# Weight units in seventeen homes, tokens gathered for two experts at once, and a hinted loop over pairs

## The chip, the cores and the metric

The kernel runs on one core of a Trainium2 chip. The metric is the device time of one execution in microseconds (us). Several executions are timed and their median is reported. One more execution is recorded by the hardware profiler; its trace covers the span from the first to the last instruction.

## The reference

One layer of a diffusion backbone, in float32, for 128 context tokens and 256 latent tokens of width 1024: a state-space mixer with a gated linear unit, then a mixture of experts, then a final norm. The change lies in the mixture of experts:

```
scores = sigmoid(t @ router_w)                 # 384 tokens, 16 experts
top_w, top_idx = two experts for each token    # both from one group of four
g = t @ w_gate[e];  u = t @ w_up[e]            # each 1024 x 1024
y += combine[e] * ((silu(g) * u) @ w_down[e])  # 1024 x 1024
x = x + g2 * y;  out = rms_norm(x) * norm_final
```

All sixteen experts are evaluated, each on those tokens that chose it. Their weights are 16 x 3 matrices of 4 MiB. The 384 tokens make 768 choices, so an expert has 48 tokens on average.

## The kernel before, in words

There is no scheduler: each engine has its own program, and counting semaphores order them. The code is named by its functions and lines.

**Weights.** An expert's weights are 12 units of 1 MiB, each loaded by two DMAs of 512 KB from SP's queue. Units 0 to 7 hold 128 rows of `w_gate` and of `w_up`; units 8 to 11 hold 256 rows of `w_down`. They live in `ring`, which has twelve slots (L102), unit u of every expert in slot u. TensorE raises `unit_free` after its last use of a unit, in the order 0 to 11 (in `expert`, L1327 to L1374), and SP's `load_unit` (L430) then loads the next expert's unit into that slot. Before the loop starts, SP loads all of E0 and also five units of E1 (0 to 4) into memory that other data has left (`early_unit`, L228, `load_early`, L450). VectorE copies these five into the ring when E0 has used the slots (L1879 to L1882), and SP goes on with unit 5. Experts are called E0 to E15 here.

**TensorE's loop** (L1400) runs over sixteen experts. Up to 96 tokens of an expert are held as three tiles of 32; the third is computed only if the expert has more than 64. One pass of `expert` does this, in order:

1. if over 64: the third tile's gate and up (`third_gate_up`) over all units 0 to 7;
2. gate and up of tiles 0 and 1, unit by unit, each 32 tokens by 512 columns on a quarter of the array (`gate_up`, L1307);
3. the first part of the gather for the next expert (`gather_x`, L1295, its five first k of eight);
4. transposes of the activations (L1357);
5. the rest of the gather;
6. if over 64: the third tile's down; then the down of tiles 0 and 1 (`down`, L1314), which use units 8 to 11.

**The gather** turns token rows into columns: for each of eight blocks k of 128 channels, three matmuls with a 128x128 block of `h2` as weights and 96 columns of a one-hot matrix (`onehot`) moved. VectorE makes the one-hot matrix (`find_tokens`, L1772) and copies the result from two PSUM banks into `xgT` (`evict_x`, L1838). E0's gather stands before the loop (`gather_first`, L1376).

**Rows out.** ScalarE applies SiLU and copies transposes; ScalarE and VectorE copy the down results into `yrow`; GpSimd scatters these to a scratch tensor `y2_scratch` in HBM. The last expert's rows stay on the chip: after the loop TensorE spreads them to tokens with matmuls (L1421).

**The end.** When the rows of E14 are sent, SP reloads the scratch in six DMAs (`load_y2`, L471), behind the weights on the same queue. ScalarE weights the first choice of each third of the tokens (`first_choice`, L845), VectorE adds the second, the gate and the residual in three steps of 1024 columns each (`other_choice`, L1843). VectorE's program has these behind its products of E15; ScalarE's has the first of them before, and the other two after, the copies of E15's last down results. Then come `combine` (L1909), the norm and the stores. If any expert had over 96 tokens, further rounds would run (L1403 on); TensorE jumps over that code.

Of the kernel before, what the change touches and what calls it, by code (L numbers as in the profile page):

```python
# [71 lines left out]
NU = 12  # L72
MAGIC = 12582912.0
# [12 lines left out]
def build(nc, x_prompt, x_sample, c, state_re, state_im, c_ctx, norm_mix, norm_ffn, w_ada, b_ada,  # L86
# [7 lines left out]
    with ctx:  # L94
# [71 lines left out]
        def cut(region, n):  # L166
# [46 lines left out]
        onehot = cut(vreg, NT * CAP).rearrange("p (t n) -> p t n", t=NT)  # L213
# [3 lines left out]
        xgT = cut(vreg, KT * CAP).rearrange("p (k t) -> p k t", k=KT)  # L217
# [6 lines left out]
        sig = cut(vreg, 512)  # L224
        prod = cut(vreg, 512)
        gfin = cut(vreg, D)
        assert off[0] <= 2 * DG * NP_V * GS
        early_unit = [mod2[:, 0, :, :].rearrange("p r n -> p (r n)"), mod2[:, 1, :, :].rearrange("p r n -> p (r n)"),  # L228
                      h2T[:, :, :].rearrange("p k t -> p (k t)")[:, 0:UNIT],
                      tmat[:, :, :].rearrange("p g n -> p (g n)"), front[:, :]]  # L230
        yo = ring[:, 8:10, :].rearrange("p a b -> p (a b)")[:, 0:NT * D].rearrange("p (t n) -> p t n", t=NT)
        y2c = [mod2[:, :, :, :].rearrange("p a r n -> p (a r n)")[:, 0:NT * D].rearrange("p (t n) -> p t n", t=NT),
               h2T[:, :, :].rearrange("p k t -> p (k t)").rearrange("p (t n) -> p t n", t=NT)]
# [5 lines left out]
        def back_of(t, j):  # L239
# [41 lines left out]
        st_zero, dve_oh_last, pe_oh_last, act_oh_last, dve_pre, pe_back, dve_oh_none, dve_mix = (sem(n) for n in (  # L281
            "st_zero", "dve_oh_last", "pe_oh_last", "act_oh_last", "dve_pre", "pe_back", "dve_oh_none", "dve_mix"))
        ld_early = [sem(f"ld_early{u}") for u in range(len(early_unit))]
# [27 lines left out]
        def first_piece(half, k):  # L311
            return ring[:, FIRST_UNITS[4 * half + k // 2], 1024 * (k % 2):1024 * (k % 2) + 1024].rearrange(
                "p (s n) -> p s n", s=2)

# [9 lines left out]
        def _(sp):  # L324
# [105 lines left out]
            def load_unit(u, e):  # L430
                if u < KT:
                    for h, w in enumerate((w_gate, w_up)):
                        sp.dma_start(ring[:, u, h * D:(h + 1) * D],  # L433
                                     w[0, bass.ds(e, 1), u * P:(u + 1) * P, :].rearrange("a p n -> (a p) n")
                                     ).then_inc(ld_unit[u], 16)
                else:
                    for h in range(2):
                        k = 2 * (u - KT) + h
                        sp.dma_start(ring[:, u, h * D:(h + 1) * D],
                                     w_down[0, bass.ds(e, 1), k * P:(k + 1) * P, :].rearrange("a p n -> (a p) n")  # L440
                                     ).then_inc(ld_unit[u], 16)

            sp.wait_ge(pe_yT, 6)
            for u in (0, 1, 5):
                load_unit(u, 0)
            for n, u in enumerate((2, 3, 6, 7, 8, 9, 10, 11, 4)):
                sp.wait_ge(glu_free, min(n + 1, KT))
                load_unit(u, 0)

            def load_early(u):  # L450
                for h, w in enumerate((w_gate, w_up)):
                    sp.dma_start(early_unit[u][:, h * D:(h + 1) * D], w[0, 1, u * P:(u + 1) * P, :]
                                 ).then_inc(ld_early[u], 16)
            load_early(4)
            sp.wait_ge(dve_x1, 6)
            load_early(3)
            sp.wait_ge(dve_h2, 6)
            load_early(0)
            load_early(1)
            sp.wait_ge(pe_logit, NT)  # L460
            load_early(2)
            for u in range(len(early_unit), NU):
# [1499 lines left out]
```

## Time and profile before

| | |
|---|---|
| median of 3 runs | 830.61 us (828.04 to 834.56) |
| the profiled execution | 827.5 us, span 825.8 us |
| mean granted clock of TensorE | 0.953 |
| TensorE matmul, weight load busy | 748.5 us (91%), 413.5 us (50%) |
| VectorE, ScalarE, GpSimd busy | 311.3 (38%), 187.7 (23%), 46.6 (6%) |
| DMA, mean over the span | 261.05 MB, 316 GB/s |

In a window row the busy times are those of TensorE, its weight loads, VectorE, ScalarE and GpSimd, in this order. The expert loop takes the span from 320.9 us to 798.3 us. Shares of the whole span mix stages with different limits, so the stages are read one at a time, with windows (busy time in a stretch) and with the instructions in order of time. Each float32 matmul shows as two matmul records and two weight-load records. Four matmuls on quarters of the array run side by side, so 128 records of them are 32 in a row.

### The profile page before, as it was taken

The page shows a single profiled execution, that of the slowest core. Times are in us where ns is not written, and L with a number is a line of the kernel's source. Part 1 is how long each engine was busy: PE and PEld are TensorE (multiplying, and loading weights), DVE is VectorE, ACT ScalarE, POOL GpSimd, SP SyncE. Part 2 cuts the span into 40 slices and gives each one's busy share as a digit, 9 for nine tenths or more (in the row PEclk, how much of TensorE's full clock was granted, in tenths as well). Part 3 has the DMA queues.
Part 4 walks back from the last instruction along what each step waited for, and adds up shares of the span by engine and source line. Part 5 has one row for each costly group of instructions (what it writes and reads, how often), then busy time and mean ns, then how long its engine had stood idle before and what let it go on. Part 6 is the DMA issues. An engine that isn't in the chain of part 4 may idle for free.

```text
span 825.8 us, 22906 instructions
## 1 busy us (share of the span) xinstructions
PE 748.5 (91%) x9776; PEld 413.5 (50%) x9777; DVE 311.3 (38%) x808; ACT 187.7 (23%) x394; POOL 46.6 (6%) x102
## 2 busy tenths in 40 slices
PE   6999788689899979999998999999999999999862
PEld 6455454484554466554552654454554554454232
DVE  6779869996022176211120211111201211121138
ACT  5535330210141133212220212201201212220132
POOL 2000300000010002100000000000000000000000
PEclk9999998959999977999999999999999999999986
DMA  9920569910059991799999999999999999999981
GB/s 329 393 80 2 204 219 397 373 40 35 22 188 348 324 376 48 272 413 409 411 410 411 410 411 411 410 410 411 410 410 379 412 410 410 411 410 410 410 332 77
DMA packets 73227, 261.05 MB, mean 316 GB/s; under 512 B 10668, under 2 KB 10716, under 8 KB 70104
## 3 DMA queue, kind: packets, MB, share of 16 engines
q1 hardware_dynamic: 71032, 257.17, 79.5%
q0 software_dynamic: 1552, 2.99, 0.9%
q8 instruction: 40, 0.66, 0.3%
q10 hardware_dynamic: 592, 0.14, 0.1%
q14 instruction: 11, 0.09, 0.0%
HBM read 252.49 MB, written 9.17 MB: 317 GB/s over the span
## 4 chain that ended last, share of the span: by engine, by line
PE 66%; DVE 16%; DMA 8%; SPq 6%; issue 3%; ACT 1%; DVEq 0%; ACTq 0%
PE ps L1311 23%; PE ps L1318 11%; PE ps L1303 8%; PE ps L1217 7%; DMA ring<-in_moe_w_up 6%; SPq L433 5%; DVE sreg L1678 3%; PE ps L1277 3%; PE ps L1153 3%; DVE scan_t L1670 3%; DMA vreg<-y_scratch 2%; PE ps L1033 2%; PE ps L1090 2%; DVE sreg L1559 2%; PE ps L1378 1%
## 5 line engine op out<-in xcount | busy, mean ns | idle before, releaser
L1311 PE MATMUL ps<-ring,vreg 128*32 128x512 f32 x2240 | 245.6, 593 | 13.1 <-DMA ring<-in_moe_w_up 8.3
L1311 PEld LDWEIGHTS ps<-ring,vreg 128*32 128x32 f32 x2240 | 72.3, 110 | 179.4 <-issue 160.9
L1318 PE MATMUL ps<-ring,vreg 128*32 128x256 f32 x2240 | 125.8, 383 | 0.8 <-ACT vreg L857 0.8
L1855 DVE TENSOR_TENSOR vreg<-vreg,ps 128x256 f32<-128x256 f32 x48 | 17.3, 417 | 212.2 <-ACT vreg L852 212.2
L1318 PEld LDWEIGHTS ps<-ring,vreg 128*32 128x32 f32 x2240 | 71.4, 111 | 49.1 <-issue 2.9
L1303 PEld LDWEIGHTS ps<-vreg,sreg 128*128 128x128 f32 x720 | 82.7, 192 | 12.6 <-issue 12.6
L1303 PE MATMUL ps<-vreg,sreg 128*128 128x96 f32 x720 | 86.0, 276 | 0.0
L1873 DVE COPY vreg<-ps 32x256 f32<-32x256 f32 x90 | 38.1, 423 | 99.6 <-PE ps L1318 97.2
L874 ACT ACTIVATE vreg<-ps 32x256 f32<-32x256 f32 x90 | 33.6, 373 | 139.4 <-PE ps L1318 137.6
L852 ACT ACTIVATE vreg<-ps 128x256 f32<-128x256 f32 x48 | 15.0, 385 | 196.3 <-PE ps L1311 196.3
L1217 PE MATMUL ps<-ring 128*128 128x512 f32 x128 | 57.8, 610 | 1.5 <-issue 0.7
L1678 DVE TENSOR_TENSOR sreg<-sreg,scan_t 128x128 f32<-128x128 f32 x190 | 47.9, 313 | 2.1
L1033 PE MATMUL ps<-ring,sreg 128*128 128x512 f32 x96 | 43.6, 601 | 1.0 <-DVE sreg L1591 1.0
L1217 PEld LDWEIGHTS ps<-ring 128*128 128x128 f32 x128 | 24.5, 194 | 31.2 <-issue 30.1
L1670 DVE TENSOR_TENSOR scan_t<-a,sreg 128x256 f32<-128x256 f32 x95 | 38.4, 445 | 1.1
L1840 DVE COPY vreg<-ps 128x480 f32<-128x480 f32 x16 | 10.5, 658 | 71.9 <-PE ps L1303 69.5
L1153 PE MATMUL ps<-sreg,vreg 64*64 64x32 f32 (+1 forms) x1024 | 25.3, 265 | 5.9 <-issue 3.6
L1033 PEld LDWEIGHTS ps<-ring,sreg 128*128 128x128 f32 x96 | 17.5, 190 | 22.5 <-issue 22.0
L1153 PEld LDWEIGHTS ps<-sreg,vreg 64*64 64x64 f32 x1024 | 24.1, 180 | 8.3 <-issue 6.1
L1277 PE MATMUL ps<-ring 128*128 128x512 f32 x64 | 27.6, 592 | 0.0
L571 POOL TENSOR_TENSOR pool_tick<-ident 1x1 f32<-1x1 f32 x30 | 5.5, 183 | 388.1 <-DVE vreg L1873 308.8
L1713 DVE TENSOR_TENSOR vreg<-vreg,ps 128x512 f32<-128x512 f32 x4 | 2.8, 688 | 52.2 <-DMA sreg<-in_x_prompt 38.0
(306 smaller groups left out, 642.3 us busy)
## 6 DMA issues: line engine op xcount, KB each, us to landing
ring<-in_moe_w_down SPq DMA_DIRECT2D x128, 512.0 KB, 12.1
ring<-in_moe_w_gate SPq DMA_DIRECT2D x123, 512.0 KB, 13.1
ring<-in_moe_w_up SPq DMA_DIRECT2D x123, 512.0 KB, 14.3
ring<-in_w_ada SPq DMA_DIRECT2D x16, 1024.0 KB, 7.5
ring<-in_w_ada SPq DMA_DIRECT2D x16, 512.0 KB, 11.8
ring<-in_ssm_w_glu SPq DMA_DIRECT2D x8, 1024.0 KB, 12.9
ring<-in_ssm_w_in SPq DMA_DIRECT2D x8, 512.0 KB, 12.3
y_scratch<-sreg SPq DMA_DIRECT2D x6, 512.0 KB, 7.1
```

What stands on the lines that cost most here:

```text
L433: sp.dma_start(ring[:, u, h * D:(h + 1) * D], w[0, bass.ds(e, 1), u * P:(u + 1) * P, :].rearrange("a p n -> (a p) n")).then_inc(ld_unit[u] ...
L874: act.activation(yrow[32 * t:32 * t + 32, 256 * j:256 * j + 256], src, ACT.Copy).then_inc(y_ev, 1)
L1033: last = pe.matmul(ps[4 + m % 4][:, :], hT[:, k, (m // 2) * P:(m // 2 + 1) * P], win[:, k, (m % 2) * 512:(m % 2 + 1) * 512], start=(k == 0 ...
L1153: last = pe.matmul(y_out(bank_of(i), i, n, o, cols), v, states_of(a, d, r, g, first_col - 1 + 2 * d, cols), start=False, stop=(d == 1 and ...
L1217: last = pe.matmul(ps[GLU_BANK[m] + part][:, :], lhs, ring[:, GLU_SLOT[k], col:col + 512], start=(k == 4), stop=(k == 3))
L1277: last = pe.matmul(ps[GLU_BANK[m] + part][:, :], yT_lat[:, k, P:2 * P], ring[:, GLU_SLOT[k], col:col + 512], start=(k == 4), stop=(k == 3))
L1303: last = pe.matmul(bank[:, col * CAP:(col + 1) * CAP], h2[:, t, k * P:(k + 1) * P], onehot[:, t, :], start=(t == 0), stop=(t == NT - 1))
L1311: last = pe.matmul(ps[t][32 * j:32 * j + 32, :], xgT[:, k, 32 * t:32 * t + 32], w[:, :, 256 * j:256 * j + 256], start=(k == 0), stop=(k == ...
L1318: last = pe.matmul(ps[3 + t // 2][32 * dj:32 * dj + 32, 256 * (t % 2):256 * (t % 2) + 256], aT[:, t, c2, 32 * j:32 * j + 32], ring[:, KT + ...
L1670: step(tt(scan_t[:, st, :, :].rearrange("p x (d g) -> p x d g", d=2), A4, chunk_states(f[st] - 1, b[st] + 1, "xdg"), ALU.mult), False)
L1678: step(tt(to, to, tb, ALU.add), False)
L1873: cp(yrow[32 * t:32 * t + 32, 256 * j:256 * j + 256], src).then_inc(y_ev, 1)
```

## The change

Three things are edited, and what depends on them.

- **Homes.** Units 0 to 6 keep one slot each in the ring. Units 7 to 11 get two homes: the ring for even experts, and for odd experts the memory that had held the early units (`odd_unit`), with semaphores of their own. That is seventeen homes. Ahead of the loop SP loads E0 and units 7 to 11 of E1, with the same waits as the early units had. In the loop SP loads units 7 to 11 of an expert first (their home was used by the expert two before) and then 0 to 6. VectorE's copies are gone. Of unit 8 the second half is loaded first. The reload of the rows goes to ring slots 8 to 10, the outputs are built in slots 0 and 1.
- **Gather.** TensorE's loop runs over eight pairs, with both experts written out in its body. A one-hot matrix for two experts (192 columns) is moved at once: half of the eight k in the even expert of a pair, the other half in the odd one, for the next pair. E0 and E1 are still gathered one by one; E1's gather stands in E0, followed by a wait until VectorE has copied it out. The last pair gathers nothing. VectorE copies out in four copies a pair, each when the odd expert has used the k that it overwrites.
[...]

The diff at its core (the rounds after the first, and signatures that only pass `odd` on, are left out):

```diff
+SINGLE = 7
+PAIRS = NE // 2
...
+        odd_unit = [front[:, :], tmat[:, :, :].rearrange("p g n -> p (g n)"),
+                    mod2[:, 0, :, :].rearrange("p r n -> p (r n)"), mod2[:, 1, :, :].rearrange("p r n -> p (r n)"),
...
+        def unit_of(u, odd):
+            return odd_unit[u - SINGLE] if odd and u >= SINGLE else ring[:, u, :]
+        yo = ring[:, 0:2, :].rearrange("p a b -> p (a b)")[:, 0:NT * D].rearrange("p (t n) -> p t n", t=NT)
+        y2c = [ring[:, 8:11, :].rearrange("p a b -> p (a b)")[:, c * NT * D:(c + 1) * NT * D].rearrange(
+            "p (t n) -> p t n", t=NT) for c in range(2)]
...
+            def load_unit(u, i, odd):
+                def of_pair(w):
+                    return w[0].rearrange("(i two) p n -> two i p n", two=2)[int(odd), bass.ds(i, 1)]
+                for h in ((1, 0) if u == KT else (0, 1)):
+                    if u < KT:
+                        src = of_pair((w_gate, w_up)[h])[:, u * P:(u + 1) * P, :]
...
+                        src = of_pair(w_down)[:, k * P:(k + 1) * P, :]
+                    sp.dma_start(unit_of(u, odd)[:, h * D:(h + 1) * D], src.rearrange("a p n -> (a p) n")
+                                 ).then_inc(landed(u, odd), 16)
...
+            load_unit(7, 0, True)
...
+            def load_both(before, i, odd):
+                for u in range(SINGLE, NU):
+                    sp.wait_ge(unit_free, before + (int(odd) * NU + u + 1 - 2 * NU))
+                    load_unit(u, i, odd)
+                for u in range(SINGLE):
+                    sp.wait_ge(unit_free, before + (int(odd) * NU + u + 1 - NU))
+                    load_unit(u, i, odd)
+            for u in range(SINGLE):
                 sp.wait_ge(unit_free, u + 1)
-                load_unit(u, 1)
-            with sp.Fori(2, NE) as e:
-                for u in range(NU):
-                    sp.wait_ge(unit_free, e * NU + (u + 1 - NU))
-                    load_unit(u, e)
+                load_unit(u, 0, True)
+            with sp.Fori(1, NE // 2) as i:
+                for odd in (False, True):
+                    load_both(i * (2 * NU), i, odd)
...
+            def gather_one():
+                for k in range(KT):
                     bank, col = (ps[5], k) if k < 5 else (ps[6], k - 5)
                     for t in range(NT):
                         last = pe.matmul(bank[:, col * CAP:(col + 1) * CAP], h2[:, t, k * P:(k + 1) * P],
                                          onehot[:, t, :], start=(t == 0), stop=(t == NT - 1))
-                if end == KT:
+                last.then_inc(xt_ps, 1)
+
+            def gather_two(k0, end):
+                for k in range(k0, end):
+                    col = k % 2 * 2 * CAP
+                    for t in range(NT):
+                        last = pe.matmul(ps[5 + k % 4 // 2][:, col:col + 2 * CAP], h2[:, t, k * P:(k + 1) * P],
+                                         pair_hot[:, t, :], start=(t == 0), stop=(t == NT - 1))
+                if end % 4 == 0:
                     last.then_inc(xt_ps, 1)
...
+            def wait_unit(u, it, two, odd):
+                if u < SINGLE:
+                    pe.wait_ge(ld_unit[u], it * 32 + 32)
+                else:
+                    pe.wait_ge(landed(u, odd), two * 16 + 32)
...
-                with pe.If(e < NE - 1):
-                    gather_x(it + 1, 0, 5)
+                    wait_unit(k, it, two, odd)
+                    gate_up(k, 0, odd)
+                    gate_up(k, 1, odd).then_inc(unit_free, 1)
+                if not odd:
+                    with pe.If(i < 1):
+                        pe.wait_ge(oh_ready, r * (PAIRS + 1) + 2)
+                        gather_one()
+                        pe.wait_ge(single_ev, r * 2 + 2)
+                with pe.If(i < PAIRS - 1):
+                    if odd:
+                        pe.wait_ge(xt_ev, two * 2 + 6)
+                    else:
+                        pe.wait_ge(oh_ready, r * (PAIRS + 1) + i + 3)
+                    gather_two(4 * int(odd), 4 * int(odd) + 3)
...
-                with pe.If(e < NE - 1):
-                    gather_x(it + 1, 5, KT)
+                with pe.If(i < PAIRS - 1):
+                    gather_two(4 * int(odd) + 3, 4 * int(odd) + 4)
...
-            with pe.Fori(0, NE) as e:
-                n = pe.value_load(counts[0:1, bass.ds(e, 1)], min_val=0, max_val=T)
-                expert(e, e, n)
+            with nc.Fori(0, PAIRS, engines=[pe.engine], hint_back_edge=True) as i:
+                for odd in (False, True):
+                    n = pe.value_load(counts[0:1, bass.ds(i * 2 + int(odd), 1)], min_val=0, max_val=T)
+                    expert(0, i, odd, n)
...
+            def find_pair(e):
+                tt(pair_hot.rearrange("p t (e n) -> p t e n", e=2),
+                   posm[:, :, bass.ds(e, 2)].rearrange("p t (e n) -> p t e n", n=1).to_broadcast((P, NT, 2, CAP)),
+                   slot_no.rearrange("p (a b n) -> p a b n", a=1, b=1).to_broadcast((P, NT, 2, CAP)), ALU.is_equal
+                   ).then_inc(oh_ready, 1)
+
+            def evict_one(gathers, m, done):
+                dve.wait_ge(xt_ps, gathers)
+                cp(xgT[:, 0:5, m, :], ps[5][:, 0:5 * CAP].rearrange("p (k n) -> p k n", k=5)).then_inc(done, 1)
+                cp(xgT[:, 5:8, m, :], ps[6][:, 0:3 * CAP].rearrange("p (k n) -> p k n", k=3)).then_inc(done, 1)
+
+            def evict_two(gathers, k0, used):
+                dve.wait_ge(xt_ps, gathers)
+                for b in range(2):
+                    k = k0 + 2 * b
+                    dve.wait_ge(unit_free, used + k + 2)
+                    cp(xgT[:, k:k + 2, :, :], ps[5 + b][:, 0:4 * CAP].rearrange("p (k e n) -> p k e n", k=2, e=2)
+                       ).then_inc(xt_ev, 1)
 
             def other_choice(t, loads):
...
+            def even_expert(it, gathers=None):
+                products(it)
+                if gathers is not None:
+                    evict_one(gathers, 1, single_ev)
+                expert_rows(it)
+
+            def odd_expert(it, gathers, units, pair=None):
+                evict_two(gathers + 3, 0, units)
+                products(it)
+                evict_two(gathers + 4, 4, units)
+                if pair is not None:
+                    find_pair(pair)
+                expert_rows(it)
+            even_expert(0, 2)
+            with dve.Fori(0, PAIRS - 2) as i:
+                odd_expert(i * 2 + 1, i * 2, i * (2 * NU) + NU, i * 2 + 4)
+                even_expert(i * 2 + 2)
+            odd_expert(NE - 3, NE - 4, NU * (NE - 3))
+            even_expert(NE - 2)
+            products(NE - 1)
+            expert_rows(NE - 1, True)
```

## Rows read from the trace of the kernel before

**Rows 1.** five stretches: us, busy (records) by engine, granted clock, DMA share, GB/s

```profile
315.00:320.00 5.00, 4.49 (x25) 4.24 (x24) 2.43 (x9) 0.47 (x1) 0.00 (x0) 0.65 0.00 0
...
342.00:348.00 6.00, 6.00 (x112) 3.38 (x104) 0.39 (x2) 0.00 (x0) 0.18 (x1) 1.00 0.65 216
...
440.00:472.00 32.00, 31.52 (x386) 16.59 (x390) 2.66 (x7) 2.01 (x6) 0.36 (x2) 1.00 1.03 410
...
592.00:630.00 38.00, 37.68 (x443) 18.57 (x438) 5.08 (x13) 5.41 (x13) 1.47 (x4) 1.00 1.00 394
...
790.00:795.00 5.00, 5.00 (x72) 2.54 (x68) 0.00 (x0) 0.00 (x0) 0.00 (x0) 0.71 1.03 411
```

**Rows 2.** waits: engine, line, awaited: total us, times, longest

```profile
PE ps L1311 <- DMA ring<-in_moe_w_up: 8.3, 9, 1.8
```

**Rows 3.** order of time, E2: start, us, engine, line, records [idle before]

```profile
375.79 13.94 PE L1311 MATMUL ps<-ring,vreg 128*32 128x512 f32 x128 [0.28 <-issue]
...
389.66 3.59 PE L1303 MATMUL ps<-vreg,sreg 128*128 128x96 f32 x30
...
393.08 0.82 PE L1357 MATMUL ps<-ident,vreg 128*128 128x128 f32 x6
...
393.74 2.15 PE L1303 MATMUL ps<-vreg,sreg 128*128 128x96 f32 x18
...
395.82 7.11 PE L1318 MATMUL ps<-ring,vreg 128*32 128x256 f32 x128
...
403.19 0.64 PE L1311 MATMUL ps<-ring,vreg 128*32 128x512 f32 x4 [0.26 <-issue]
```

**Rows 4.** order of time, TensorE: experts with more than 64 tokens (E4, E9)

```profile
440.20 14.80 PE L1311 MATMUL ps<-ring,vreg 128*32 128x512 f32 x136 [1.79 <-DMA ring<-in_moe_w_up]
...
461.09 10.57 PE L1318 MATMUL ps<-ring,vreg 128*32 128x256 f32 x192
...
471.93 3.64 PE L1311 MATMUL ps<-ring,vreg 128*32 128x512 f32 x32 [0.28 <-issue]
...
592.31 20.81 PE L1311 MATMUL ps<-ring,vreg 128*32 128x512 f32 x192
```

**Rows 5.** order of time, TensorE, last expert

```profile
784.67 1.92 PE L1311 MATMUL ps<-ring,vreg 128*32 128x512 f32 x16 [0.64 <-DMA ring<-in_moe_w_up]
...
789.53 8.75 PE L1318 MATMUL ps<-ring,vreg 128*32 128x256 f32 x128 [0.80 <-ACT vreg L857]
```

**Rows 6.** order of time, chain of waits: matmuls before the loop

```profile
292.73 3.64 PE L1264 MATMUL ps<-sreg,vreg 128*128 128x16 f32 x32
...
250.82 13.73 PE ps L1217 x32
```

**Rows 7.** order of time, last steps before the loop, first after

```profile
319.20 0.66 DVE L1840 COPY vreg<-ps 128x480 f32<-128x480 f32 x1 [2.40 <-PE ps L1378]
...
320.87 13.94 PE L1311 MATMUL ps<-ring,vreg 128*32 128x512 f32 x128 [1.38 <-DVE vreg L1841]
...
797.46 1.15 ACT L847 ACTIVATE sreg<-sreg,cmb 128x1024 f32<-128x1024 f32 x1 [8.23 <-DMA vreg<-y_scratch]
...
803.70 1.15 ACT L847 ACTIVATE sreg<-sreg,cmb 128x1024 f32<-128x1024 f32 x1 [2.54 <-DMA vreg<-y_scratch]
...
803.89 5.50 PE L1421 MATMUL ps<-vreg,oh_rep 32*128 32x256 f32 x48 [5.60 <-issue]
...
808.73 1.23 DVE L1850 TENSOR_TENSOR sreg<-sreg 128x1024 f32<-128x1024 f32 x1
```

**Rows 8.** order of time, SP's queue: first loads after the seventeen

```profile
331.43 0.33 SPq L433 DMA_DIRECT2D ring<-in_moe_w_gate  x1
...
342.89 6.18 SPq L439 DMA_DIRECT2D ring<-in_moe_w_down  x8
```

**Rows 9.** the page: engine totals, instruction queue

```profile
PE 748.5 (91%) x9776; PEld 413.5 (50%) x9777; DVE 311.3 (38%) x808; ACT 187.7 (23%) x394; POOL 46.6 (6%) x102
...
q8 instruction: 40, 0.66, 0.3%
```

More of the change, by code:

```diff
@@ L313, in first_piece, with landed @@
                 "p (s n) -> p s n", s=2)
+        def landed(u, odd):
+            return ld_odd[u - SINGLE] if odd and u >= SINGLE else ld_unit[u]
         def of_half(i):
@@ L1294, in _ @@
                       start=False, stop=True, skip_group_check=True).then_inc(pe_pos, 1)
-            def gather_x(nth, first, end):
-                if first == 0:
-                    pe.wait_ge(oh_ready, nth + 1)
-                for k in range(first, end):
+            def gather_one():
+                for k in range(KT):
                     bank, col = (ps[5], k) if k < 5 else (ps[6], k - 5)
@@ L1335, in expert @@
-            def expert(it, e, count=None):
-                pe.wait_ge(xt_ev, it * 2 + 2)
+                        wait_unit(KT + kk // 2, it, two, odd)
+                    down(kk, 2, odd)
+            def expert(r, i, odd, count=None):
+                it = r * NE + i * 2 + int(odd) if count is None else i * 2 + int(odd)
+                two = r * NE + i * 2 if count is None else i * 2
+                pe.wait_ge(xt_ev, two * 2 + 4)
                 pe.wait_ge(prod_done, it * TT + TT)
                 if count is None:
-                    third_gate_up(it)
+                    third_gate_up(it, two, odd)
@@ L1363, in expert @@
                 if count is None:
-                    third_down(it)
+                    third_down(it, two, odd)
                 else:
                     with pe.If(count > 64):
-                        third_down(it)
+                        third_down(it, two, odd)
                 for kk in range(KT):
                     if kk % 2 == 0:
-                        pe.wait_ge(ld_unit[KT + kk // 2], it * 32 + 32)
-                    down(kk, 0)
-                    last = down(kk, 1)
+                        wait_unit(KT + kk // 2, it, two, odd)
+                    down(kk, 0, odd)
+                    last = down(kk, 1, odd)
                     if kk % 2:
@@ L1406, in _ @@
                     pe.wait_ge(xt_ev, r * (2 * NE))
-                    gather_x(r * NE, 0, KT)
-                    with pe.Fori(0, NE) as e:
-                        expert(r * NE + e, e)
+                    pe.wait_ge(oh_ready, r * (PAIRS + 1) + 1)
+                    gather_one()
+                    with nc.Fori(0, PAIRS, engines=[pe.engine], hint_back_edge=True) as i:
+                        for odd in (False, True):
+                            expert(r, i, odd)
                 pe.wait_ge(y_ev, 12 * NE * ROUNDS + 12)
@@ L1850, in other_choice, with products @@
                 tt(m, m, x1[:, t, :], ALU.add).then_inc(dve_pre, 1)
-            def expert(it, next_but_one, last_of_round=False, last=False):
+            def products(it):
                 for t in range(TT):
@@ L1855, in expert, with expert_rows @@
                     tt(act_a[:, t, :], sg[:, t, :], ps[t][:, 256:512], ALU.mult).then_inc(prod_done, 1)
[L1856 to L1859 removed]
+            def expert_rows(it, last=False):
                 if last:
@@ L1875, in _ @@
             dve.sem_inc(y_ev, 11)
-            evict_x(0)
+            evict_one(1, 0, xt_ev)
+            dve.sem_inc(xt_ev, 2)
             find_tokens(1)
+            find_pair(2)
             slot_numbers()
-            for u in range(len(early_unit)):
-                dve.wait_ge(ld_early[u], 32)
-                dve.wait_ge(unit_free, u + 1)
-                cp(ring[:, u, :], early_unit[u]).then_inc(ld_unit[u], 32)
-            with dve.Fori(0, NE - 2) as e:
-                expert(e, e + 2)
-            expert(NE - 2, None)
-            expert(NE - 1, None, True, True)
+            def even_expert(it, gathers=None):
[18 more added lines that the diff above has]
+            expert_rows(NE - 1, True)
             v = dve.value_load(cmaxi[0:1, 0:1], min_val=0, max_val=T)
```

114 lines of the change are left out of this document (43 added, 71 removed).

## The prediction

> **What bounds the kernel now.** I read the granted clock and DMA share by stretch first, then TensorE's waits, then the order of time on TensorE and on SP's queue. The expert loop is full on two resources at once. [...] TensorE's waits for weights add up to only 8.3 us over sixteen experts [rows 2]. DMA is idle just before the loop (nothing moves from 315 to 320) and a third idle from 342 to 348 [rows 1]. So what one resource gains can be taken back by the other, and both must be followed to the end.
>
> An expert of at most 64 tokens is 27.4 us of TensorE: gate and up 13.9, gather 3.5, transposes 0.7, gather 2.0, down 7.0, 0.3 of loop [rows 3]. Three experts (the fifth, eighth and tenth; I number them E4, E7, E9, from E0) have over 64 and take 10.4 more: 20.8 for 13.9, 10.6 for 7.1 [rows 3, 4]. One expert's weights are 12 units of 1 MiB. **Pace of the stream:** the last gate/up unit of E4 is used at 440.20 and that of E15 at 784.67, 132 units later [rows 4, 5]: 344.5 us. From 592 to 630 the DMA engines moved 394 GB/s for 410 [rows 1], a hole of 1.5 us. Without it 343.0/132 = 2.60 us a unit, the scatters of rows included, or 31.2 us an expert. An average expert of TensorE is 27.4 + 3 x 10.4/16 = 29.4. Weights are therefore the scarcer thing, and at the end of the loop TensorE waits for each unit.
>
> **The change part by part.**
>
> *Gather for two.* A 128x128 weight load with 16 columns moved takes 3.64/32 = 114 ns a record, and with 96 columns 3.59/30, that is 117 [rows 3, 6]: the load sets the time. Moving sets it for 512 columns (13.73/32 = 429 ns) and for 256 (four side by side, 4 x 7.11/128 = 222) [rows 3, 6]. For 192 columns: 192/512 x 429 = 161 or 192/256 x 222 = 167; the ends are 117 (the load still hides it) and 234 (two of today's). I take 167, the nearest width. A pair then costs 48 x 0.167 = 8.0 us for 11.0, half in each expert: a small expert falls from 27.4 to 26.0 (3.0 + 1.0 for 3.5 + 2.0). E0 carries in addition the single gather for E1 (48 x 0.117 = 5.6) and TensorE's new wait until DVE has emptied its two banks. Such an eviction took from 319.20 to the restart at 320.87, 1.7 us with the count's load [rows 3, 7]; I take 1.4. Behind that wait stand the pair's gather and E0's transposes and down; VectorE is free by then. E0 becomes 26.0 + 5.6 + 1.4 = 33.0. The last pair gathers nothing: E14 is 22.0. TensorE alone would end at 320.9 + 33.0 + 10 x 26.0 + 3 x 36.4 + 22.0 + 25.6 = 770.7, where 25.6 is E15's 13.9 and the 11.7 from its gates' end (784.67 + 1.92) to 798.28 [rows 5]. The loop ends at 798.3 now.
>
> *Seventeen homes.* As many units (17) are loaded ahead of the loop as before; VectorE's five copies go, and it has room anyway. What moves is the next load. Today unit 5 of E1 is issued at 331.43, after six units of E0 are used, and unit 8 of E1 at 342.89, after E0's first down unit; then the stream runs on with 20 units issued before it [rows 8]. After: unit 0 of E1 can go at 320.9 + 1.7 = 322.6, 8.8 us earlier. Eight units (0 to 6 of E1, 7 of E2) keep DMA busy to about 345. Unit 8 of E2 needs E0's first down unit, and E0 is longer: 320.9 + 13.9 + 5.6 + 1.4 + 3.0 + 0.7 + 1.0 + 1.9 = 348.4. DMA is idle for some 4 us, then runs on with 25 units behind it. The lead is 5 x 2.60 - (348.4 - 342.9) = 7.5 us. From then on I find no late home: the tightest are the down homes after the large experts, free 4 us before DMA wants them, so the 1.5 us hole goes too. The stream ends 9 us earlier.
>
> *The order of loads.* This takes it back. An expert's units 7 to 11 are now loaded before its 0 to 6. Today the stream's last gate unit is number 188 of 192 (7 of E15); after, the last of all is unit 6 of E15, and its gates stand behind it. By position: today's lag is 440.20 - 342.89 - 36 x 2.60 = 3.7; unit 6 of E15 is the 167th of the restarted stream, 348.4 + 167 x 2.60 + 3.7 = 786.3. I call this landing L15; each earlier expert's is 31.2 less: L4 443.1, L7 536.7, L9 599.1, L12 692.7, L13 723.9, L14 755.1.
> TensorE against it: E4 starts at 320.9 + 33.0 + 3 x 26.0 = 431.9 and wants unit 6 at 437.1; it waits 6.0 and ends at 443.1 + 31.2 = 474.3 (today 471.93). E7 wants it 5.2 too soon, E9 and E12 just in time, E13, E14 and E15 wait about 5 us each. From L15 remain unit 6's gates (1.7), unit 7's (1.9) and 11.7: the last down ends at 786.3 + 15.3 = 801.6, against 798.3. The gather's 20 us have become waits; this row of waits grows from 8 us to 25 or 30.
>
> *The end.* Today the reload of the rows lands behind the last weights: ScalarE takes up the first third at 797.46 and the last at 803.70, and VectorE ends the second choice at 810.0, 11.7 after the last down [rows 7]. After, it still queues behind the weights, but these end at 786: the first third is weighted under E15's down. Two remain, behind ScalarE's copies of the last rows: 1.0 + 1.2, then 6 x 1.23 = 9.6 after the last down. TensorE's first products start 5.6 after the last down [rows 5, 7] and are two thirds done when wanted. So 2.1 are won. The code that TensorE jumps over there grows; that idle time can go from 5.6 to twice that, which would cost 4.
>
> **Sum.** 825.8 + 3.3 - 2.1 = 827.0 of span. The profiled execution took 827.5 with 1.7 outside the span, 3.1 under the median of the runs (830.61) and just under the lowest of them. So 828.7 for such an execution and 832 for the median, with the same 3.1.
>
> *The hint and the bigger loop body.* TensorE's body today is about 900 instructions (a matmul is two loads and two matmul records) and passes its back edge with 0.3 us idle [rows 3]. Queue 8 brought instructions 40 times, 0.66 MB [rows 9], 16 KB each. [...] The new body is about 1,850. [...]
> [...]
>
> **Rivals.**
> *Slower: the back edge misses in spite of the hint.* Seven edges of F us. TensorE alone ends at 770.7 + 7F, and the stream holds the end at 801.6, so F under 4.4 costs next to nothing. At 5.6 the last down ends at 809.9, the span at 835.3, the median at 840. It passes 1% from F = 5.4 on, or from less if the exit misses too. For it: the body doubles. [...] Chance 0.18, dips of the clock included: it fell to 0.71 after E15's waits and the down took 8.75 us for 7.11 [rows 1, 3, 5]; longer waits could cost E15 another 2 to 5.
> *Faster: the stream does better.* The pace without scatters is 1.049 MB/410 GB/s = 2.56. If scatters go free, 167 x 0.04 = 7 us; if the hole at 345 closes as well, 4 more. The end is 827.0 - 11 = 816, the median 821. For it: fewer late homes. Against: the pace was the same wherever DMA was full. Chance 0.10.
> *Faster: TensorE is the bound.* Then its 770.7 would show: span about 796, median 801. Only if weights came 20 us earlier than their bytes allow. Chance 0.03.
> *The gather gains nothing (234 ns).* E1 to E13 1.6 us longer each, the end still that of the stream: no change of the sum. Inside the forecast.
>
> **Numbers.** Forecast 0.69: lag and pace (0.01 us a unit is 1.7 us) and the exit give its own range, 825 to 838. With 1% of the median (8.3 us) as what can be told from no change: faster 0.11, same 0.72, slower 0.17, since an edge of each neighbour stays within 1%. The range 821 to 843 leaves out the TensorE-bound case and the worst misses.
>
> **What would show it.** Right: 16-DMA share full from about 349 to 786 with an idle patch before it; the first ring load of E1 at 322.6; pair gathers of some 167 ns a record; waits for weights of 5 to 6 us in E4 and in the gates of E13 to E15; last down near 801; three other-choice rows ending near 811. Wrong: idle of several us at the start of even experts (the hint failed); a stream that pauses again after E4, E7 or E9 (homes late); the last down well under 798 (my order-of-loads step fails); a unit pace off 2.60.

## The result, and the profile after

The changed kernel takes 832.76 us (median of 18 runs, 830.35 to 837.63) against 830.31 for the kernel before on the same chip: ratio 1.0039, 95% interval 1.0020 to 1.0058. The forecast was 832. The profiled execution has a span of 830.0 us.

The order of time on TensorE shows the change at work in E2, which took 27.4 us before [rows 3]. Columns: start, us, engine, line, records, and the idle time before them.

```profile
384.18 13.94 PE L1326 MATMUL ps<-ring,vreg 128*32 128x512 f32 x128 [0.45 <-issue]
...
409.84 1.47 PE L1326 MATMUL ps<-ring,vreg 128*32 128x512 f32 x12
```

E2 is now 409.84 - 384.18 = 25.7 us. But at the end of the loop the gates now follow the stream unit by unit. Before, only the last four gate units of E15 were late, by 3.1 us in all (the last of them in [rows 5]); now it is seven of its eight, by 6.0:

```profile
775.04 1.92 PE L1326 MATMUL ps<-ring,vreg 128*32 128x512 f32 x16 [1.64 <-DMA ring<-in_moe_w_up]
...
788.37 1.92 PE L1326 MATMUL ps<-ring,vreg 128*32 128x512 f32 x16 [0.62 <-DMA ring<-in_moe_w_up]
790.93 1.92 PE L1326 MATMUL ps<-ring,vreg 128*32 128x512 f32 x16 [0.64 <-DMA ring<-in_moe_w_up]
792.67 1.90 PE L1326 MATMUL ps<-front,vreg 128*32 128x512 f32 x16
...
797.51 1.93 PE L1333 MATMUL ps<-tmat,vreg 128*32 128x256 f32 x32 [0.81 <-ACT vreg L867]
...
802.71 1.91 PE L1333 MATMUL ps<-vreg 128*32 128x256 f32 x32
808.13 5.50 PE L1456 MATMUL ps<-vreg,oh_rep 32*128 32x256 f32 x48 [3.50 <-issue]
```

The last down ends at 802.71 + 1.91 = 804.6, the span 25.4 later. The waits of the gates' line, 8.3 us before [rows 2], have become (engine, line, awaited: total us, times, longest)

```profile
PE ps L1326 <- DMA ring<-in_moe_w_up: 22.5, 26, 1.8
```

and the stretches of the changed kernel (us, busy time by engine, granted clock, DMA share, GB/s) show a full stream around an idle patch, beside [rows 1]:

```profile
344.00:346.00 2.00, 2.00 (x7) 2.00 (x7) 0.00 (x0) 0.00 (x0) 0.00 (x0) 0.50 0.82 326
346.00:348.00 2.00, 2.00 (x15) 1.98 (x15) 0.00 (x0) 0.63 (x2) 0.00 (x0) 0.96 0.08 31
348.00:350.00 2.00, 1.85 (x29) 1.04 (x30) 0.00 (x0) 0.24 (x1) 0.00 (x0) 1.00 0.03 8
...
352.00:354.00 2.00, 2.00 (x44) 1.19 (x40) 0.00 (x0) 0.00 (x0) 0.00 (x0) 1.00 0.89 320
400.00:440.00 40.00, 39.24 (x466) 20.23 (x464) 8.97 (x20) 9.72 (x21) 2.14 (x6) 1.00 1.03 410
...
740.00:785.00 45.00, 35.13 (x406) 12.06 (x398) 6.17 (x15) 7.56 (x18) 2.74 (x7) 1.00 1.03 409
```

From 400 to 440 two resources are full at once, TensorE busy 39.24 of 40 us at a granted clock of 1.00 and DMA at 410 GB/s, as in [rows 1] from 440 to 472. In the last stretch TensorE is busy 35 of 45 us and waits 7.6 for weights (4.4 in the same stretch before), while DMA never pauses: what the gather gave is spent waiting.

### The profile page after: what moved, and what is told of

It reads as the page before. It is cut to its first block, busy times and chain, and to the rows that moved or that the text cites. A ratio compares the mean times of both kernels' runs of the same rounds, so it can differ in the third digit from the quotient of the medians.

```text
span 830.0 us, 22220 instructions
## 1 busy us (share of the span) xinstructions
PE 734.8 (89%) x9440; PEld 390.5 (47%) x9441; DVE 306.4 (37%) x796; ACT 187.4 (23%) x394; POOL 44.3 (5%) x102
## 4 chain that ended last, share of the span: by engine, by line
PE 58%; DMA 13%; DVE 10%; issue 2%; SPq 2%; ACT 1%; DVEq 0%; ACTq 0%
PE ps L1326 22%; DMA ring<-in_moe_w_up 13%; PE ps L1333 12%; PE ps L1227 7%; PE ps L1318 6%; DVE sreg L1713 3%; PE ps L1287 3%; PE ps L1163 3%; DVE scan_t L1705 3%; SPq L448 2%; PE ps L1410 1%; PE ps L1389 1%; PE ps L1171 1%; PE ps L1310 1%; DVE sreg L1982 0%
## 5 line engine op out<-in xcount | busy, mean ns | idle before, releaser
L1326 PE MATMUL ps<-ring,vreg 128*32 128x512 f32 x2096 | 236.7, 600 | 28.2 <-DMA ring<-in_moe_w_up 22.5
L1326 PEld LDWEIGHTS ps<-ring,vreg 128*32 128x32 f32 x2096 | 65.3, 110 | 191.1 <-issue 142.1
L1318 PE MATMUL ps<-vreg,sreg 128*128 128x192 f32 x336 | 62.3, 337 | 1.6 <-DVE vreg L1882 1.6
L1333 PE MATMUL ps<-ring,vreg 128*32 128x256 f32 x1088 | 60.8, 380 | 1.1 <-ACT vreg L867 0.8
L1318 PEld LDWEIGHTS ps<-vreg,sreg 128*128 128x128 f32 x336 | 55.6, 194 | 12.7 <-issue 12.7
L1333 PEld LDWEIGHTS ps<-ring,vreg 128*32 128x32 f32 x1088 | 34.6, 110 | 25.7 <-issue 3.6
L1889 DVE COPY vreg<-ps 128x384 f32<-128x384 f32 x28 | 15.0, 556 | 70.3 <-PE ps L1326 47.2
L1333 PE MATMUL ps<-sreg,vreg 128*32 128x256 f32 x576 | 32.9, 379 | 0.0
L1043 PEld LDWEIGHTS ps<-ring,sreg 128*128 128x128 f32 x96 | 17.5, 190 | 22.5 <-issue 22.0
## 6 DMA issues: line engine op xcount, KB each, us to landing
tmat<-in_moe_w_down SPq DMA_DIRECT2D x16, 512.0 KB, 10.4
```

What stands on the lines that cost most here:

```text
L1043: last = pe.matmul(ps[4 + m % 4][:, :], hT[:, k, (m // 2) * P:(m // 2 + 1) * P], win[:, k, (m % 2) * 512:(m % 2 + 1) * 512], start=(k == 0 ...
L1318: last = pe.matmul(ps[5 + k % 4 // 2][:, col:col + 2 * CAP], h2[:, t, k * P:(k + 1) * P], pair_hot[:, t, :], start=(t == 0), stop=(t == NT ...
L1326: last = pe.matmul(ps[t][32 * j:32 * j + 32, :], xgT[:, k, int(odd), 32 * t:32 * t + 32], w[:, :, 256 * j:256 * j + 256], start=(k == 0), ...
L1333: last = pe.matmul(ps[3 + t // 2][32 * dj:32 * dj + 32, 256 * (t % 2):256 * (t % 2) + 256], aT[:, t, c2, 32 * j:32 * j + 32], unit_of(KT + ...
```

## The experiments

Two theories. **O**: the stream sets the end, and the new order of loads (units 7 to 11 of an expert before its 0 to 6) puts the last gates behind the last byte. **T**: TensorE sets it, through the gather, the bigger body or its back edge. Since the part before the loop varies by some us between profiled executions (E0 starts from 318.69 to 327.21), I compare from E0's start: the last down ends 477.4 later before, 483.6 after. Intervals are of the ratio to the kernel before, on the same chip.

**1. Last expert's loads in the order of use.**

```
-            with sp.Fori(1, NE // 2) as i:          # all pairs
+            with sp.Fori(1, NE // 2 - 1) as i:      # all but the last
...
+            load_both(last * (2 * NU), last, False)
+            for u in range(SINGLE):       # E15: 0 to 6 first, then 7 to 11
+                sp.wait_ge(unit_free, last * (2 * NU) + u + 1)
+                load_unit(u, last, True)
+            for u in range(SINGLE, NU):
+                sp.wait_ge(unit_free, last * (2 * NU) + u + 1 - NU)
+                load_unit(u, last, True)
```

> The changed kernel, but for the last expert (E15) units 0 to 6 are loaded before 7 to 11; all other experts as changed. Theory O (the order of loads gives the stream's lead back): the stream still ends at about 791, but now with unit 11. Unit 7 of E15 lands four places earlier, at 790.9 - 4 x 2.6 = 780.5, its gates end at 782.4, the last down at 793 to 794 (804.6 in the changed kernel). The reload of the rows lands at 793.5 to 798.7 and now bounds VectorE; the span is about 822, 8 us under the changed kernel (830.0) and 4 under the kernel before (825.8). Rival T (TensorE's own work or the end after the loop sets the time): the last down moves by less than 2 us, the span stays at 828 to 830.

828.43 us, 0.9965 (0.9937 to 0.9992). The last down ends 476.3 after E0's start, 7.3 earlier than after. The order of time on TensorE, E14's gates to E15's:

```profile
762.04 3.64 PE L1334 MATMUL ps<-ring,vreg 128*32 128x512 f32 x32 [0.64 <-DMA ring<-in_moe_w_up]
...
768.63 8.66 PE L1341 MATMUL ps<-ring,vreg 128*32 128x256 f32 x128 [0.81 <-ACT vreg L875]
777.12 12.21 PE L1334 MATMUL ps<-ring,vreg 128*32 128x512 f32 x112
```

E15 no longer waits for weights; the end is now set one expert earlier, by E14's own unit 6, and behind it stands all of E15. O is right in kind, and the step was a third smaller than I expected because the same order acts in E14 too.

**2. That order for every expert.**

```
+                for u in range(SINGLE):
+                    sp.wait_ge(unit_free, before + (int(odd) * NU + u + 1 - NU))
+                    load_unit(u, i, odd)
                 for u in range(SINGLE, NU):
                     sp.wait_ge(unit_free, before + (int(odd) * NU + u + 1 - 2 * NU))
                     load_unit(u, i, odd)
-                for u in range(SINGLE):
...
```

> The changed kernel with units 0 to 6 loaded before 7 to 11 for every expert. Theory O: the gain at E15 is the same (about 10 us between the stream's end and the last down), but the early stream pays: after E1's units 0 to 6 the queue must wait for E1's gates to free unit 0 (about 360) where the changed kernel went on at 350.8 with the down units, so the stream is 9 us and one unit (2.6) later, 11.7. Last down 803 to 806, span 829 to 833. Rival: if order alone mattered and the homes were never late, the span would be near 820.

834.33, 1.0033 (1.0000 to 1.0066), as expected: the last down ends 482.1 after E0's start, and the gain at the end and the loss at the start cancel. SP now waits before E2's loads for E1's gates: it issues the first of them 37.1 us after E0's start (364.34), where the changed kernel's go 29.9 after it (350.82) and with one unit more ahead of them. The order that costs 7 us at the end buys a fuller stream at the start.

**3. Order of use from E4 on.** SP's loop runs over pairs 2 to 7 with units 0 to 11 in turn.

```
-            with sp.Fori(1, NE // 2) as i:
+            with sp.Fori(1, 2) as i:
...
+            with sp.Fori(2, NE // 2) as i:
+                for odd in (False, True):
+                    for u in range(NU):
+                        old = 1 if u < SINGLE else 2
+                        sp.wait_ge(unit_free, i * (2 * NU) + (int(odd) * NU + u + 1 - old * NU))
+                        load_unit(u, i, odd)
```

> The changed kernel, but from E4 on every expert's units are loaded in the order in which TensorE uses them, 0 to 11; E2 and E3 keep 7 to 11 first, so E0's early down homes are still used. Times from E0's start, since it varies between profiles. Theory O: the stream ends as in the changed kernel (its last landing 470 after E0's start), but with unit 11; neither E14 nor E15 has its gates behind the last landings, so the last down ends 3 us after the stream, at 473 to 475 (changed kernel 483.6, the kernel with only E15 reordered 476.3, kernel before 477.4). The rows' reload then sets the end, 12.8 after the stream: span 5 us under the kernel with only E15 reordered, ratio to the kernel before about 0.99. Rival: the loads in use order find their homes late at the switch (E4's unit 0 needs E3's gates) and the stream has a hole of 5 us or more there; then no more than the gain of the E15 order alone is left.

827.88, 0.9962 (0.9930 to 0.9994): level with experiment 1. The last down came when expected (473.4), but the last weights now land under the last downs and the reload of rows queues behind them. ScalarE's order of time:

```profile
801.83 1.15 ACT L863 ACTIVATE ring<-ring,cmb 128x1024 f32<-128x1024 f32 x1 [8.86 <-DMA ring<-y_scratch]
...
804.32 1.15 ACT L863 ACTIVATE ring<-ring,cmb 128x1024 f32<-128x1024 f32 x1 [0.59 <-DMA ring<-y_scratch]
...
806.81 1.15 ACT L863 ACTIVATE ring<-ring,cmb 128x1024 f32<-128x1024 f32 x1 [1.34 <-DMA ring<-y_scratch]
```

In the changed kernel the first of these is done at 798.2, before the last down. The tail is 29.5 for 25.4. What the order wins, the reload gives back.

**4. The same, with the next pair's gathers behind E0's down** (in every even expert), to fill the patch near 350.

```
+                if not odd:        # behind down(), was ahead of the transposes
+                    with pe.If(i < 1):
+                        pe.wait_ge(oh_ready, r * (PAIRS + 1) + 2)
+                        gather_one()
+                        pe.wait_ge(single_ev, r * 2 + 2)
+                    with pe.If(i < PAIRS - 1):
+                        pe.wait_ge(oh_ready, r * (PAIRS + 1) + i + 3)
+                        gather_two(0, 4)
```

> The previous variant, and in every even expert the gathers stand behind the down instead of between gates and down (E0: E1's gather, its wait and the pair's gather). Its transposes are no longer covered, about 2 us more of TensorE in each even expert, which the stream hides. E0's first down unit comes at about 17 us after E0's start instead of 28, so units 8 to 11 of E2 are issued without a hole; the next wait is for E1's first gates, at about 38 to 41 after E0's start with 30 units issued (29.9 with 25 in the changed kernel). Theory (the hole after E0 delays the whole stream): 2 to 5 us under the previous variant. Rival (only the last experts count): no difference beyond 1 us.

832.34, 1.0017 (0.9993 to 1.0042): some 5 us worse than experiment 3, where I expected 2 to 5 better. E0's down starts at 337.99, and the down units of E2 follow without a pause. But the patch isn't filled, it moves. E2's first gates have to wait for E1's, and the stream, 5.5 us idle in experiment 3 (352.9 to 358.4), idles 4.2 here (357.0 to 361.2). The gathers no longer cover the evictions between gates, transposes and down in even experts (in E0 0.95 us of wait before each of the two), so E4 starts 3.1 us later from E0's start. E4's loads in order of use wait for E3's gates and leave a second pause of 3.4 us (412.2 to 415.6). Filling the hole isn't a gain if it takes a cover away.

**5. 250 columns moved where 192 are used.**

```
-  last = pe.matmul(ps[...][:, col:col + 2 * CAP], ..., pair_hot[:, t, :], ...)
+  last = pe.matmul(ps[...][:, col:col + WIDE], ..., moved(t), ...)   # WIDE = 250
```

> The changed kernel with 250 columns moved in each of the pair gather's matmuls instead of 192 (58 surplus columns, overwritten or not read), so that 24 records cost 1.2 us an expert more at the same number of instructions: body 1,980 instructions; the variant with narrow matmuls had 2,076. Theory (from E4 on the stream bounds; the narrow variant's 70 us were missed branch targets and not gather time): span within 2 us of the changed kernel's, 830 to 832; no idle of 10 us at the edges. Rival (TensorE's gather is on the path): 14 x 1.2 = 17 us, span 847.

834.34, 1.0052 (1.0023 to 1.0080), and the last down at 482.8 for 483.6. The E1 gather of the two kernels, the changed one first:

```profile
371.75 3.19 PE L1318 MATMUL ps<-vreg,sreg 128*128 128x192 f32 x18
...
375.44 1.14 PE L1318 MATMUL ps<-vreg,sreg 128*128 128x192 f32 x6
```

```profile
374.01 4.06 PE L1322 MATMUL ps<-vreg,sreg 128*128 128x250 f32 x18
...
378.56 1.43 PE L1322 MATMUL ps<-vreg,sreg 128*128 128x250 f32 x6
```

From this gather's start to the transposes behind it, that is 3.90 for 3.03. Over thirteen experts some 15 us of TensorE moved the time by 2 or less. The waits for weights gave 8.5 of it, from 22.5 to 14.0. Most of the rest is that this run was spared two stretches of low clock: its first pair gather took 4.06 us like all later ones, where the changed kernel's took 4.87 for 3.19, and E4's gates behind their waits took 15.66 for 18.51.

**6. Half the bytes of each weight unit from E2 on.**

```
+  cols = D if isinstance(i, int) else D // 2
-  sp.dma_start(unit_of(u, odd)[:, h * D:(h + 1) * D], src...)
+  sp.dma_start(unit_of(u, odd)[:, h * D:h * D + cols], src[:, 0:cols])
```

> The changed kernel with only 512 of the 1024 columns of every weight row loaded from E2 on (the rest of each unit is stale), so the stream needs half the time and TensorE alone bounds. Theory: the last down ends where TensorE's own sum puts it, 772.8 - 320.9 = 452 us after E0's start (10 small experts of 25.75, 3 of 36.2, edges of 0.4), against 483.6; span about 798. This is what the gather is worth if weights come for free. Rival (waits for VectorE or ScalarE, not for weights, hold TensorE in E4 and E13 to E15): the span stays above 815.

801.83 (two runs), 0.9645 (0.9595 to 0.9694): no wait for weights is left, and the last down ends 452.7 after E0's start. 31 us of the changed kernel's time is the stream's.

**7. Experiments 5 and 6 together.**

> The run with half of every weight row (801.0), and 250 columns moved in the pair gather instead of 192. TensorE bounds here, so the 1.2 us that 24 wider records cost should all show: 14 x 1.2 = 17, span 816 to 819, where the same edit cost 1 to 2 us with the full stream. Rival (the gather is hidden by something else than the stream): under 805.

815.77, 0.9815 (0.9771 to 0.9859): 13.6 us from E0's start over experiment 6. The same edit that was hidden under the full stream shows nearly whole once the stream is light. That is the plainest evidence for O over T.

**8. The hint off.** Both places of `hint_back_edge=True`, an argument of TensorE's loops over pairs, set to False.

> The changed kernel with hint_back_edge=False on the loops over pairs. Theory F (the back edge misses without the hint, 3 to 6 us each): the even experts from E2 on start 3 to 6 us after the last down before them, but as the stream bounds, only what exceeds 3.8 us an edge shows at the end: span 830 to 838. Rival R (the body of some 1,850 instructions stays on the engine whole, the hint has nothing to save): the idle at the edges stays at 0.3 to 0.5 us, the instruction queue brings 42 blocks as now, span 829 to 831.

901.87, 1.0884 (1.0815 to 1.0954), far from either figure. The order of time at the first back edge, and the waits of TensorE:

```profile
379.73 1.91 PE L1333 MATMUL ps<-vreg 128*32 128x256 f32 x32
392.23 4.50 PE L1326 MATMUL ps<-ring,vreg 128*32 128x512 f32 x20 [10.59 <-issue]
```

```profile
PE ps L1326 <- issue: 75.0, 11, 11.0
PE ps L1333 <- issue: 6.8, 4, 2.5
```

```profile
q8 instruction: 106, 1.74, 0.8%
```

Against the changed kernel, whose three rows are

```profile
PE ps L1326 <- issue: 4.3, 8, 1.7
...
PE ps L1333 <- issue: 0.2, 1, 0.2
```

```profile
q8 instruction: 42, 0.69, 0.3%
```

it waits 70.7 + 6.6 us more for instructions and fetches 64 more blocks of 16 KB (1.74 MB for 0.69), nine a back edge. The matmuls add 746.1 - 734.8 = 11.3, as the clock stands at 0.65 in the gap (381 to 392) and at 0.70 in the 10 us after it. All of the 22.5 of waiting for weights is gone. 70.7 + 6.6 + 11.3 - 22.5 = 66.1; the spans differ by 66.3.

**9. The hint off with half the bytes.**

> The changed kernel with half of every weight row loaded from E2 on (as in the run with half the weights, 801.0 of span) and no hint. Every microsecond of TensorE shows here. Theory Q (the missed branch costs what a fetch costs once it has waited behind the weights' transfers, 10.6 us at E1's end with the stream full): with the stream busy half the time an edge costs 4 to 6 us, seven of them 28 to 42: span 829 to 843. Rival (the miss has a fixed price of 10 to 11): 801 + 7 x 10.2 = 872 or more.

861.48 (two runs), 1.0365 (1.0312 to 1.0419), between the two expectations. TensorE's waits for instructions, where experiment 6 has 2.6 us in all:

```profile
PE ps L1328 <- issue: 46.8, 9, 8.0
```

That is 44.2 us more or 6.3 an edge, against (70.7 + 6.6)/7 = 11.0 with the full stream; the first miss is 8.00 for 10.59. So a good half of a miss is there with the stream at half its bytes, and the full stream adds the rest. With nothing to hide behind, all of it shows: the spans differ by 55.9 us, the 44.2 and 13.6 more of matmuls at the lower clock (0.923 over the span for 0.945).

**10. The hint kept, the body lengthened.** Each 192-column gather as two of 96.

```
-  last = pe.matmul(..., pair_hot[:, t, :], ...)
+  for e in range(2):      # CAP = 96 columns each
+      for t in range(NT):
+          last = pe.matmul(..., pair_hot[:, t, e * CAP:(e + 1) * CAP], ...)
```

> The changed kernel with each 192-column gather matmul written as two of 96 columns, as dear as the gather before (48 x 0.117 us more work per expert half, 1.4 us an expert). Theory (the stream bounds from E4 on, TensorE's saving only became waits): E1 to E13 are 1.4 us longer each and their waits shorter by as much; the stream is later only by what E0's first down unit is later, 0.7 to 1.4 us. Span 830.5 to 832. Rival (TensorE bounds): 13 x 1.4 = 18 us, span 848.

906.29, 1.0928 (1.0862 to 1.0993). I expected next to nothing to show. TensorE's waits and the fetches:

```profile
PE ps L1328 <- issue: 66.1, 8, 10.7
```

```profile
q8 instruction: 107, 1.75, 0.8%
```

The same picture as without the hint: all seven edges wait, 7.9 to 10.7 us each. Counted in the compiled programs, from the first instruction of the loop to its branch back, TensorE's loop body is 905 instructions before, 1,815 after and 1,911 here. (The expectation of experiment 5 has 1,980 and 2,076, each 165 too many.) The difference of 96 is the 24 added matmuls, each two loads and two matmuls. So 1,911 misses at each edge even with the hint, and 1,815 only without it. What decides between the two is not shown by any run.

**11. The last pair's loads in order of use**, to keep what experiments 1 and 3 won.

```
-            with sp.Fori(1, NE // 2) as i:
+            with sp.Fori(1, NE // 2 - 1) as i:
...
+            last = NE // 2 - 1
+            for odd in (False, True):
+                for u in range(NU):
+                    old = 1 if u < SINGLE else 2
+                    sp.wait_ge(unit_free, last * (2 * NU) + int(odd) * NU + u + 1 - old * NU)
+                    load_unit(u, last, odd)
```

> The changed kernel, but both experts of the last pair (E14 and E15) have their units loaded in the order of use, 0 to 11. In the variant with E15 alone reordered, E15 no longer waited, but E14 still had its gates behind its own unit 6, and the last down ended 476.3 after E0's start (changed kernel 483.6, kernel before 477.4). Theory O: with E14 reordered too its gates are not held, E15's unit 7 lands 10.4 before the stream's end, and the last down ends at 473 to 474. The reload of the rows then lands too late to be hidden and costs 2 to 3, so the span is 2 us under the E15 variant, 500 after E0's start; the ratio to the kernel before is 0.992 to 0.995. Rival (E14's early units find late homes): no better than the E15 variant, 0.9965.

823.34, 0.9914 (0.9884 to 0.9944), as expected: under both kernels, by an interval clear of 1, though by less than 1%. The last down ends 473.2 after E0's start, 10.4 earlier than after. E14 and E15 on TensorE:

```profile
744.79 13.94 PE L1332 MATMUL ps<-ring,vreg 128*32 128x512 f32 x128 [0.41 <-issue]
...
768.61 12.20 PE L1332 MATMUL ps<-ring,vreg 128*32 128x512 f32 x112
...
785.76 3.18 PE L1339 MATMUL ps<-tmat,vreg 128*32 128x256 f32 x32 [0.81 <-ACT vreg L873]
```

Neither waits for weights. The tail grows from 25.4 to 27.8, since the reload lands late as in experiment 3, so 8.0 of the 10.4 are kept. The last down still runs partly at a fallen clock: 8.8 us (785.76 to 794.56, granted 0.81) for 7.1.

## Why the prediction was right, point by point

**The sum.** Predicted: last down 801.6, span 827.0. Measured: 804.6 and 830.0, both 3.0 late. That the median came out within 1 us of the forecast is in part luck: the profiled execution was taken as 3.1 under the median and was 1.1 under it, which hides 2 of the 3. The steps, from L15 back and forward:

- *Gather.* 167 ns a record taken; 3.03/18 = 168 measured, start to start (371.75 to the transposes at 374.78). A small expert 26.0 taken, 25.7 to 26.3 measured. Right.
- *E0.* 33.0 taken, 357.88 - 320.97 = 36.9 measured. TensorE's order of time:

```profile
334.84 5.60 PE L1310 MATMUL ps<-vreg,sreg 128*128 128x96 f32 x48
342.03 4.87 PE L1318 MATMUL ps<-vreg,sreg 128*128 128x192 f32 x18 [1.59 <-DVE vreg L1882]
...
348.68 7.52 PE L1333 MATMUL ps<-ring,vreg 128*32 128x256 f32 x128 [0.15 <-issue]
357.88 1.50 PE L1326 MATMUL ps<-ring,vreg 128*32 128x512 f32 x12 [1.68 <-issue]
```

  The mis-sized terms: the pair's first gather and the first downs run at a fallen clock (0.50 from 343 to 346; the gather took 4.87 for the later 3.19, the down 7.52 for 7.11: 2.1 us), and the first passage into E1 idles 1.68 where I had 0.3. The eviction wait was 1.59 for 1.4.
- *Homes.* The first load of E1 is issued at 322.95 (322.6 taken) and unit 8 of E2 at 350.82 (348.4), late by 1.7 of clock and smaller delays. SP's queue:

```profile
322.95 0.33 SPq L448 DMA_DIRECT2D ring<-in_moe_w_gate  x1
...
350.82 2.44 SPq L448 DMA_DIRECT2D ring<-in_moe_w_down  x3
```

  The stream idles some 5 us (4 taken), then runs on; [rows 1]'s dip near 592 to 630 is gone (410 GB/s there). The stream ends some 4 us earlier than before, for 9 taken. Before, unit 7 of E15 is used at 784.67 [rows 5] with four units behind it, 784.67 + 4 x 2.61 = 795.1; after, the last unit of all is used at 790.93.
- *Pace.* Unit 6 of E4 is used at 446.17 and unit 6 of E15 at 790.93: 344.76/132 = 2.61 a unit for 2.60 taken.
- *Order of loads.* L15 786.3 taken, 790.93 measured. 2.4 of it is the restart, about 2 the pace (167 x 0.012). So this term, with the restart, was 4.6 too small. The waits were to grow from 8 to 25 or 30 and grew to 22.5. E9 waited 0.6 and E12 1.0 in all, about the "just in time" of the prediction; E7 waited 2.5 where I had 5.2, since E4 had ended 5.4 late. Experiments 1 and 11 show the order itself to be the cause, worth 7 to 10 us.
- *After L15.* 15.3 taken, 13.7 measured. I had carried over the slow down of before, 8.75 us [rows 5]; the clock stayed at 1.00 from 790 to 805 this time. These 1.6 us made up for part of the 4.6.
- *Tail.* 25.4 taken and measured: one third of the rows was weighted early, at 797.09, and VectorE ended the second choice 9.5 after the last down (9.6 taken). The idle time at the loop's exit was 3.50, and did not grow with the code that is jumped over.

E4 ended at 479.75 for 474.3, a miss of the same kinds: 2.4 of restart and a clock of 0.70 from 446 to 456, right behind its waits (18.51 us for 144 records that took 15.6 in E7):

```profile
446.17 18.51 PE L1326 MATMUL ps<-ring,vreg 128*32 128x512 f32 x144 [1.76 <-DMA ring<-in_moe_w_up]
...
479.75 0.61 PE L1326 MATMUL ps<-ring,vreg 128*32 128x512 f32 x4
```

It cost nothing, as the stream sets what follows.

**The rivals.** *Back edge misses in spite of the hint*: they don't; the edges idle 0.24 to 0.45 us, and queue 8 brings no instructions from 384 to 790 us. But its price was badly off. The rival is reckoned at 5.6 us, the idle time at the loop's exit [rows 7], and no run shows a miss at that price with the full stream: experiments 8 and 10 show some 10.5 for the first, and all seven of experiment 8 cost 12.7 each with the slow clock behind them ((70.7 + 6.6 + 11.3)/7). The body of "about 1,850" was counted well (1,815), but that it had room to spare was my own estimate, and there was little: 96 instructions more, 1,911, miss at every edge. Had it missed, the result would have been near 900, outside my range by 57 us; I gave this rival 840. The forecast held since the edges did not miss, not since the risk was judged rightly. *Stream does better*: no, the pace was 2.61 and the patch stayed. *TensorE the bound*: its time was sized nearly rightly (in experiment 6 the last down ends 452.7 after E0's start, where this rival had 770.7 - 320.9 = 449.8, and E0 alone ran over by 3.9), and it is hidden, as said. *Gather gains nothing*: experiment 5 is nearly this case (216 ns), and the time hardly moved, as said.

**Where the gain went.** The gather gave some 1.5 us in each of E1 to E13. With E0's longer way and E14's missing gather, some 16 us of TensorE's time are left of it: experiment 6 has its last down at 452.7, and before it was at 477.4, of which 8.3 were waits for weights. They became waits, because in this loop the stream is the scarcer. The stream ended some 4 us earlier. I put that down to the homes; no run has them alone. It was taken back by the order of loads. Before, E15's last gates stood behind the 188th unit, and the last four landed under them and the downs; after, they stand behind the 192nd, so nothing is left of the stream to lie under the last down. Four units are 10.4 us, less the 4.2 of the stream makes the last down 6.3 us later (798.28 to 804.62), and the end behind it is 2.1 shorter: 4.2 us more span.

## What to carry over

Where two resources are both nearly full, follow the last byte of the scarcer one and count what stands behind its use: the order of the last loads was worth as much as a doubled gather. Count the instructions of an unrolled loop body before it is doubled, and do not rely on room for a hundred more. Here 1,815 repeated without a fetch (none on queue 8 from 384 to 790 us) and 1,911 did not, and each missed back edge cost some 10 us with the full stream, which a saving of 1.5 us an expert can't pay for. Restrict a repair to where it acts: the order of use helps in the last pair, and costs what it gains when it starts earlier.

## What the hardware showed that I had not expected

- The hint on the back edge is worth 66 us of span here (896.3 without it, 830.0 with it). A body of 1,815 instructions repeats at next to no cost with it (42 instruction fetches) and is fetched again at every edge without it (106). The 905 of before needed no hint: two of its edges idle 0.28 and 0.26 us in [rows 3], and queue 8 brings nothing from 350 to 790. Why the longer body isn't kept without it, and from which size on, is not settled by these runs.
- A gap of TensorE that comes from instructions costs more than its length: around the first one of experiment 8 the clock stood at 0.65 in it (381 to 392) and at 0.70 in the 10 us after it.
- The clock also stood at 0.50 from 344 to 346 with TensorE busy all that time: behind it lay 5.6 us of 96-column gather and a wait of 1.6 us. Experiment 4, with the same two steps ahead, took 5.84 us for 24 records there (0.79 from 350 to 358). But these two steps are not the whole cause: experiments 1, 5, 8 and 9 have them too, and ran their first pair gather at the full clock (3.19 us for 18 records, and 4.06 in experiment 5, as later on). What decides between the two is open, and its 1.7 us are noise for a forecast.
